# Head norms by token rows in the attention stage, and four smaller reorderings, in a two-layer encoder step

## The reference

```python
def _rms(x, g):
    y = xf * lax.rsqrt(jnp.mean(xf * xf, axis=-1, keepdims=True) + EPS)
    return (y * g).astype(x.dtype)
# in _diff_attention, eight heads, each 128 wide
p = jax.nn.softmax(jnp.where(mask, s + bias, NEG_BIG), axis=-1)
a = p[:, :, 0] - lam * p[:, :, 1]
o = jnp.einsum('bhqk,bkhe->bqhe', a, v_all)
o = _rms(o, head_g) * (1 - lam_init)
return o.reshape(B, T, D_MODEL) @ w_o
```

## Time and profile before

| what | us |
|---|---|
| median of three runs | 1470.3 (1469.63 to 1471.16) |
| the profiled execution | 1470.15 |
| its span, first to last instruction | 1468.4 |
| PE busy | 1444.8 |
| PEld busy | 1368.3 |
| DVE busy | 1048.7 |
| POOL busy | 759.3 |
| ACT busy | 427.6 |

### The profile page before, as it was taken

The page is one execution under the profiler, slowest core; times in us unless marked ns, Lnnn a source line. Parts: engine busy times, 40 slices in busy tenths (PEclk is TensorE's granted clock), DMA queues, the critical chain, the costliest instruction groups (busy, mean ns, idle before and its releaser), DMA issues.

```text
span 1468.4 us, 29233 instructions
## 1 busy us (share of the span) xinstructions
PE 1444.8 (98%) x11236; PEld 1368.3 (93%) x11236; DVE 1048.7 (71%) x1862; ACT 427.6 (29%) x906; POOL 759.3 (52%) x513
## 2 busy tenths in 40 slices
PE   6999999999999999999999999999999999999999
PEld 4987899999999999999999887778999999999998
DVE  5897665567776877776688347886966779476698
ACT  5303454211110011112232147774421133111132
POOL 2445343555555455555545444567565556555554
PEclk9999999999999999999999999999999999999999
DMA  9573222244456544444222252231222222222222
GB/s 377 177 254 133 89 87 74 87 157 151 166 200 214 194 144 162 153 169 138 83 92 72 84 190 89 89 103 38 79 85 73 86 94 79 89 84 86 86 90 104
DMA packets 57531, 183.50 MB, mean 125 GB/s; under 512 B 6440, under 2 KB 9904, under 8 KB 57440
## 3 DMA queue, kind: packets, MB, share of 16 engines
q1 hardware_dynamic: 54432, 179.25, 35.7%
q10 hardware_dynamic: 3008, 3.01, 0.6%
HBM read 171.69 MB, written 10.55 MB: 124 GB/s over the span
## 4 chain that ended last, share of the span: by engine, by line
PE 90%; DVE 5%; issue 1%; DMA 1%; ACT 1%; POOL 0%; SPq 0%; ACTq 0%; DVEq 0%; POOLq 0%
PE psum L779 62%; PE psum L845 7%; PE psum L1054 7%; PE psum L1253 3%; PE psum L1345 1%; PE psum L1188 1%; DMA ada_first<-in_ada_w 1%; PE psum L1308 1%; PE psum L1060 1%; DVE w_ring L2581 1%; DVE act_lo L2013 1%; PE psum L1295 1%; PE psum L1291 1%; PE psum L790 1%; PE psum L816 1%
## 5 line engine op out<-in xcount | busy, mean ns | idle before, releaser
L658 POOL TENSOR_SCALAR w_hi<-raw 128x1024 fp32r<-128x1024 f32 (+1 forms) x168 | 192.0, 1143 | 574.4 <-PE psum L779 478.3
L662 POOL TENSOR_TENSOR w_lo<-raw,w_hi 128x1024 fp32r<-128x1024 f32 (+2 forms) x195 | 440.5, 2264 | 14.0
L779 PE MATMUL psum<-act_hi,w_hi 128*128 128x288 f32 (+1 forms) x1952 | 424.8, 299 | 1.3 <-issue 0.6
L779 PE MATMUL psum<-act_hi,w_lo 128*128 128x288 f32 (+1 forms) x1952 | 420.9, 297 | 0.0
L779 PE MATMUL psum<-act_lo,w_hi 128*128 128x288 f32 (+1 forms) x1952 | 420.5, 297 | 0.0
L779 PEld LDWEIGHTS psum<-act_hi,w_hi 128*128 128x128 f32 x1952 | 315.5, 190 | 6.4 <-issue 4.0
L779 PEld LDWEIGHTS psum<-act_hi,w_lo 128*128 128x128 f32 x1952 | 316.0, 189 | 0.0
L779 PEld LDWEIGHTS psum<-act_lo,w_hi 128*128 128x128 f32 x1952 | 315.3, 189 | 0.0
L779 PE MATMUL psum<-hid_both,w_hi 128*128 128x288 f32 x704 | 122.9, 297 | 0.0
L1960 DVE SCALAR_TENSOR_TENSOR psum<-ada_quad,cst,psum 128x512 f32<-128x512 f32 x168 | 112.8, 748 | 0.0
L779 PEld LDWEIGHTS psum<-hid_both,w_hi 128*128 128x128 f32 x704 | 103.5, 189 | 1.2 <-issue 1.2
(11 more groups left out here) (383 smaller groups left out, 2457.2 us busy)
## 6 DMA issues: line engine op xcount, KB each, us to landing
raw<-in_w_stream SPq DMA_DIRECT2D x153, 512.0 KB, 3.5
ada_quad<-in_ada_w SPq DMA_DIRECT2D x56, 512.0 KB, 4.5
raw<-in_w_down SPq DMA_DIRECT2D x32, 704.0 KB, 4.1
ada_first<-in_ada_w SPq DMA_DIRECT2D x8, 1024.0 KB, 14.2
ada_ring<-in_ada_w SPq DMA_DIRECT2D x14, 512.0 KB, 4.4
ada_more<-in_ada_w SPq DMA_DIRECT2D x10, 512.0 KB, 5.3
line_rep<-line SPq DMA_DIRECT2D x8, 352.0 KB, 4.5
line<-line_rep SPq DMA_DIRECT2D x8, 352.0 KB, 5.2
```

The costliest lines, as they stand in the source:

```text
L658: pool.tensor_scalar(hi, src, 1.0, 0.0, ALU.mult, ALU.add).then_inc(hi_split, 1)
L662: last = pool.tensor_tensor(lo[:, c:c + w], src[:, c:c + w], hi[:, c:c + w].bitcast(F32), ALU.subtract)
L779: last = mm(psum[:, b + half, 0:n_cols], weights[wp][:, k, :], parts[ap][:, k, half * HT:half * HT + n_cols], start=(k == 0 and n == 0), s ...
```

## The change

**Attention.** `att_values` swaps its operands, so a head's output comes out with tokens on partitions: a block is 128 tokens by 128 features. The sum of squares is then ScalarE's own accumulation (`out_squares`: five Square instructions, then Identity, Ln and Exp on 128x5). VectorE makes the root (`out_root`, three instructions on 128x5), which stands in step 3 behind `att_score` and ahead of `att_weight`; ScalarE scales the four prompt blocks (`out_norm`), VectorE the sample block (`out_norm`, behind `att_weight`); TensorE turns the five tiles back (`out_turn`, step 4) and ScalarE copies them to SBUF (`out_back`). `att_sums`, `att_sums_sample` and GpSimd's nine instructions per head go. The heads alternate between PSUM banks 5 and 6. In the tail, `out_turn` of head 7 stands ahead of the last `out_part`, and the eight pieces of output unit 4 run in another order on other banks.

```diff
                     pool.memset(bias_p[(h + 1) % 2][0:64, 448:512], NEG).then_inc(mask_ready, 1)
                 if h == H - 1:
                     split_unit(U_AO + 3)
-                if h >= 1:
-                    z, y, t, o = (tmp[:, n, :] for n in (1, 2, 3, 5))
-                    pool.wait_ge(oy_ready, h)
-                    pool.wait_ge(oz_ready, 2 * h)
-                    if 2 <= h <= 3:
-                        pool.wait_ge(lo_ready[A_O], 1)
-                    elif h >= 4:
-                        pool.wait_ge(sc_mm, 5 * h + 5)
-                    if h == 1:
-                        pool.wait_ge(kv_stored, 192)
-                    def by_half(out, a, b):
-                        pool.tensor_tensor(out[:, 0:HT], a[:, 0:HT], b[:, 0:HT], ALU.mult)
-                        return pool.tensor_tensor(out[:, HT:T], a[:, HT:T], b[:, HT:T], ALU.mult)
-
-                    steps(by_half(t, y, y))
-                    steps.wait()
-                    steps(by_half(t, t, z))
-                    steps.wait()
-                    steps(pool.tensor_scalar(t, t, -0.5, 1.5, ALU.mult, ALU.add))
-                    steps.wait()
-                    steps(by_half(t, t, y))
-                    steps.wait()
-                    by_half(o_place[h - 1][:, :], t, o).then_inc(ov_ready, 1)
-                    pool.wait_ge(ov_ready, h)
             split_pairs(121, 2)
             def sum_blocks(hf, n):
...
-                if h >= 1:
-                    pe.wait_ge(o_out, h)
+                if qt == 0 and h >= 2:
+                    pe.wait_ge(ov_ready, h - 1)
+                if qt == 0 and 1 <= h < H - 1:
...
                     for kt in range(5):
                         n = P if kt < 4 else TS
                         w = vc_sb[h % 2][:, kt, :] if kt < 4 else v_sb[h // 4][0:TS, 4, h % 4 * P:(h % 4 + 1) * P]
-                        last = mm(psum[:, 4, 448:512], w, atr[0:n, g % 2, kt * DK:(kt + 1) * DK], start=(kt == 0), stop=(kt == 4))
+                        last = mm(psum[0:TS, 4, 384:512], atr[0:n, g % 2, kt * DK:(kt + 1) * DK], w, start=(kt == 0), stop=(kt == 4))
                 last.then_inc(av_done, 1)
 
-            def att_sums(h):
-
-                pe.wait_ge(osq_ready, h + 1)
-                pe.wait_ge(kz_ready, min(2 * H, H + h + 3))
-                if h >= 1:
-                    pe.wait_ge(oz_ready, 2 * h)
-                mm(psum[:, 6, :], mean_sq, tmp[:, 0, 0:TP], start=True, stop=True)
-
-            def att_sums_sample(h, late=False):
-
-                pe.wait_ge(o_out, h + 1)
-                pe.wait_ge(at_ready, min(5 * H, 5 * h + 6 + late))
-                mm(psum[:, 4, 448:512], mean_sq, tmp[:, 0, TP:T], start=True, stop=True).then_inc(oms_ready, 1)
+            def out_turn(h):
+
+                pe.wait_ge(hn_act, H + h + 1)
+                pe.wait_ge(hn_dve, H + h + 1)
+                pe.wait_ge(at_ready, min(5 * H, 5 * h + 7))
+                for j in range(4):
+                    pe.transpose(psum[:, o_bank(h), j * P:(j + 1) * P], hn[j], ident)
+                pe.transpose(psum[:, 4, 448:512], hn[4], ident[0:TS, 0:TS]).then_inc(o_turned, 1)
 
             def out_part(f):
...
+                elif s == 4 and p >= 1:
+                    out_turn(p - 1)
...
-            att_sums_sample(H - 1)
             for f in parts:
+                if f == 15:
+                    out_turn(H - 1)
                 out_part(f)
             pe.wait_ge(lo_split, U_AO + 5)
             pe.wait_ge(o_half_read, 12)
-            pe.wait_ge(o_out, H)
-            pe.wait_ge(oz_ready, 2 * H)
-            for k, j in ((0, 0), (0, 1), (1, 0), (1, 1), (2, 0), (3, 0), (2, 1), (3, 1)):
+            pe.wait_ge(ov_ready, H - 1)
+            for k, j in ((0, 0), (1, 0), (2, 0), (0, 1), (1, 1), (2, 1), (3, 0), (3, 1)):
                 if j == 0:
                     pe.wait_ge(lo_ready[A_O], 5 + k)
-                last = out_tile(4, j, k, 4 + 2 * j, k == 0, k == 3)
+                elif k == 0:
+                    pe.wait_ge(ov_ready, H)
+                last = out_tile(4, j, k, o_banks[j], k == 0, k == 3)
                 if (k, j) == (3, 0):
                     last.then_inc(o_done, 1)
...
             def out_sample(h):
                 sa.wait_ge(av_done, 5 * h + 5)
                 if h >= 1:
-                    sa.wait_ge(ov_ready, h)
-                af(tmp[:, 5, TP:T], psum[:, 4, 448:512], ACT.Copy)
-
-            def out_prompt(h):
-                af(tmp[:, 5, 0:TP], psum[:, 5, :], ACT.Copy).then_inc(o_out, 1)
+                    sa.wait_ge(hn_dve, H + h)
+                af(o_sample, psum[0:TS, 4, 384:512], ACT.Copy).then_inc(o_out, 1)
+
+            def out_squares(h):
                 sa.wait_ge(o_out, h + 1)
-                if h >= 1:
-                    sa.wait_ge(oms_ready, h)
-                af(tmp[:, 0, :], tmp[:, 5, :], ACT.Square).then_inc(osq_ready, 1)
-
-            def z_sample(h):
-                sa.wait_ge(oms_ready, h + 1)
-                if h >= 1:
-                    sa.wait_ge(ov_ready, h)
-                af(tmp[:, 1, TP:T], psum[:, 4, 448:512], ACT.Identity, bias=EPSC, scale=D / P).then_inc(oz_ready, 1)
-
-            def z_prompt(h):
-                af(tmp[:, 1, 0:TP], psum[:, 6, :], ACT.Identity, bias=EPSC, scale=D / P).then_inc(oz_ready, 1)
-
-            def head_guess(h):
-                sa.wait_ge(oz_ready, 2 * h + 2)
-                steps(af(tmp[:, 2, :], tmp[:, 1, :], ACT.Ln))
+                for j in range(TT):
+                    src = psum[:, o_bank(h), j * P:(j + 1) * P] if j < 4 else o_sample
+                    n = P if j < 4 else TS
+                    last = af(hn[j], src, ACT.Square, accum_out=ssq[0:n, j:j + 1])
+                steps(last)
                 steps.wait()
-                af(tmp[:, 2, :], tmp[:, 2, :], ACT.Exp, scale=-0.5).then_inc(oy_ready, 1)
+                steps(af(z5, ssq, ACT.Identity, bias=EPSC, scale=1.0 / P))
+                steps.wait()
+                steps(af(y5, z5, ACT.Ln))
+                steps.wait()
+                af(y5, y5, ACT.Exp, scale=-0.5).then_inc(oy_ready, 1)
+
+            def out_norm(h):
+                sa.wait_ge(of_ready, h + 1)
+                for j in range(4):
...
                     ts_(selr[:, h % 2, :], cst[:, C_SEL2:C_SEL2 + DK], r[:, 0:1], VEC, ALU.mult, ALU.mult).then_inc(weighted, 1)
 
+            def out_root(h):
+                ve.wait_ge(oy_ready, h + 1)
+                if h >= 1:
+                    ve.wait_ge(hn_act, H + h)
+                newton(y5, z5, t5, f5).then_inc(of_ready, 1)
+
+            def out_norm(h):
+                ve.wait_ge(of_ready, h + 1)
+                ts_(hn[4], o_sample, f5[0:TS, 4:5], None, ALU.mult).then_inc(hn_dve, 1)
+
             def head_lo(h):
                 ve.wait_ge(hi_ready[A_O], h + 1)
...
                     query_first(p + 2)
-                elif s == 4 and p + 3 < H:
+                elif s == 4 and 1 <= p < H - 3:
                     query_second(p + 2)
                 elif g == 5 * (H - 2):
                     query_second(H - 1)
+                if s == 3 and p >= 1:
+                    out_root(p - 1)
                 if g >= 1:
                     att_weight(g - 1)
+                if s == 3 and p >= 1:
+                    out_norm(p - 1)
                 if g == 3:
                     kq_scale(H + 1, tmp[:, 5, :])
+                    query_second(2)
                 elif s == 2 and 1 <= p < H - 1:
```

```diff
+            def split_behind(u0, but_last_used):
+
+                pool.wait_ge(raw_in[u0 % 2], 16 * (u0 // 2 + 1))
+                but_last_used()
+                for k0, k1 in ((0, KT - 1), (KT - 1, KT)):
+                    src = raw[:, u0 % 2, k0 * P:k1 * P]
+                    hi, lo = (w_parts[u0 % 2][part][:, k0:k1].rearrange("p k c -> p (k c)") for part in range(2))
+                    if k1 == KT:
+                        pool.wait_ge(unit_done, u0 - 1)
+                    last = pool.tensor_scalar(hi, src, 1.0, 0.0, ALU.mult, ALU.add)
+                    if k1 < KT:
+                        steps(last)
+                        steps.wait()
+                    else:
+                        last.then_inc(hi_split, 1)
+                        pool.wait_ge(hi_split, u0 + 1)
+                    if k1 < KT:
+                        pool.wait_ge(lo_ready[A_HN], H)
+                    last = pool.tensor_tensor(lo, src, hi.bitcast(F32), ALU.subtract)
+                last.then_inc(lo_split, 1)
+
...
-            split_pairs(3, 26)
+            split_pairs(3, (U_OUT - 1) // 2)
+            split_behind(U_OUT + 2, lambda: pool.wait_ge(turned, H))
+            split_unit(U_OUT + 3)
+            split_pairs(U_OUT + 4, 2)
+            split_unit(U_FFN0, pieces=4)
+            split_unit(U_FFN0 + 1)
```

(10 more changed lines are left out.)

102 lines of the change are left out of this document (45 added, 57 removed).

## The result

| | before | after |
|---|---|---|
| median | 1470.3 (1468.41 to 1471.16) | 1477.51 (1477.06 to 1479.72) |
| ratio | | 1.0052, 95% interval 1.0042 to 1.0063 |
| the profiled execution, its span | 1470.15, 1468.4 | 1479.72, 1477.9 |

The change makes the kernel 7.2 us slower; the forecast was 2.2 us, its range ended 0.5 us under the measured median. The profiled execution lies 2.2 us over its own median. S of a head is the start of TensorE's scores of step 2, as in the prediction.

The account below looks back on a forecast made before the run. It took TensorE, 90% of the chain, as the bound. Mixer -1.7, heads 1 to 4 +3.6, later heads and tail +0.4 gave +2.3 us on 1470.15: forecast 1472.5, its own range 1469.5 to 1475.5, overall 1466 to 1477.

Parts of the forecast that it names:

- the values keep their products: TensorE in a head: swapping the operands of the values was taken to leave their products as they were.
- the 1.4 named as a sign: Heads 1 to 4: TensorE's weight transposes of block 3 would wait about 1.4 us for VectorE, once a head.
- The even case of 4 x 0.48 us gained: Heads 1 to 4, in the faster rival: the root's wait is hidden, giving 4 x 0.48 us; 1463 in all, chance 0.13.
- the term of +0.85: Head 5: out_turn waits for ScalarE's scalings from S+8.7 to S+10.95, moving the turn of block 3 by +0.85 us.
- -0.3, since the wait of block 3 behind a long split piece shrinks: Head 7: the 1.2 us wait of block 3 behind a long split piece would shrink, for -0.3 us.
- the unit boundary: Tail: +0.45 us, as unit 4's first half ends 0.8 us instead of 1.6 before the second, its residual taking 1.1.
- The wait of 0.5 us that the tail was to lose: Tail: a TensorE wait of 0.5 us was to be gone, part of the tail's -0.5 us.
- The k-tile: Mixer, ahead of the heads: six products of 0.13 us each fill TensorE's wait, for -0.75 us.
- the state DMAs: Mixer: four DMA issues less ahead of ScalarE's squares bring them 1.8 us forward, for -0.2 us.
- The early split: Mixer's output units: the split of seven k-tiles starts some 4 us earlier, ending TensorE's idle 0.62 us, for -0.75 us.
- A wait that is removed can't cost: Mixer: the claim that its terms, together -1.7 us, could not turn into a loss; the gain ends at -1.8.
- the waits add up: Slower rival: out_turn late by 1.3 us or more delays block 3's turn, 2.5 us per 0.5 in five heads; 1477, chance 0.2.

Follow-up runs that it names:

- split_late: The changed kernel, with GpSimd's split in heads 1 to 4 waiting until VectorE has ended the weights of block 3: 1475.63 us.
- comb: The changed kernel with later head_hi, root, out_turn and splits of heads 1 to 4, head 7's split in four low pieces, GpSimd's mixer order of before: 1471.64 us.
- short_hold: The changed kernel, with the low part of the unit split in head 7 cut from one GpSimd instruction into four: 1475.81 us.
- both_late: The changed kernel, with head_hi of heads 5 to 7 behind step 3's scalings and the low part of head 7's split unit in four pieces: 1473.11 us.
- mixer_only: The kernel before, with the change's GpSimd and mixer parts and nothing of the attention: 1469.47 us.
- mixer_no_behind: The kernel before, with the change's mixer part only (k-tile ahead of the heads, earlier state DMAs), GpSimd's order as before: 1469.89 us.
- filler: The changed kernel, with eight repeated score products added to TensorE ahead of the long out_turn waits in each of heads 5 and 7: 1475.55 us.

## Why the prediction was right or wrong

**Heads 1 to 4: right, +3.6 forecast, +3.55 measured.** The two steps that carry it hold. The root waits for ScalarE for 1.23 us (1.15 forecast), and the low pieces run under the weights of block 3 and cost 0.64 us (0.66 forecast). So VectorE frees TensorE at S+14.39 (14.4 forecast). TensorE's own steps were off and it didn't show: `out_turn` waited 0.44 us, five transposes took 0.79 (0.65 taken; the earlier trace rows had said 0.78), and "the values keep their products" was wrong for the sample, whose products are now 128 wide and not 64: +0.16. Without any wait for block 3, as in split_late, TensorE turns it at S+13.75 and not at 13.03, so the wait there was 0.6 us and not the 1.4 named as a sign. The even case of 4 x 0.48 us gained was never there: with both causes and the wait of `out_turn` mended (comb) the four heads take 78.85 us, 0.12 a head under before. That the sum agrees to 0.05 us is luck: by the scatter of these heads it could as well have been +2.8 or +4.3. One reading was not borne out by its row: the scores at 904.14 in the earlier trace rows ran behind the split, which ended at 903.61 in the earlier trace rows, so they say nothing on whether scores are held beside it. Nothing in the sum used this.

**Head 5: the wait right, its price wrong.** The forecast of 2.25 us (10.95 less 8.7) was 2.19 measured. The step that failed is the term of +0.85: it priced a wait at its own length. With the clock up the same head takes 21.3 us (split_late), +1.15; in the profiled execution it took 22.7 (+2.6), and up to 24.2 in another kernel. The prediction read the granted clock of the earlier trace rows and took it as given for the stretches that it made idle; the runs show 1.4 us more behind this wait, for 3.4 us at half clock.

**Head 7: wrong.** "-0.3, since the wait of block 3 behind a long split piece shrinks" followed the long instruction only to the place where it had stood. With the norm's nine instructions gone from GpSimd and the scaling new on VectorE, it met the scaling. 1.6 us of wait (3.1 in the place of 1.5) and 1.35 of clock came of it, and short_hold and both_late give these 2.95 us back. The tail missed the same thing at a smaller price, 0.35 us, and the unit boundary cost 0.7 where 0.45 was taken. The wait of 0.5 us that the tail was to lose did not stand there: of the two waits for VectorE's x in the kernel before, 0.48 us lay in head 6 (at 988.12) and 0.33 in head 7 (1012.78), none in the tail.

**The mixer: -1.7 forecast, -0.6 measured.** The k-tile gave 0.59 (0.75), because its six products took 1.0 us there and not 0.8; the state DMAs gave 0.32 (0.2). The early split failed, -0.75 forecast and +0.4 measured (mixer_only against mixer_no_behind). The sentence "PE began a unit late since the split came late" was right, but what comes next was not asked. It was the residual on VectorE, 0.08 us behind, and the long low part itself made it later. "A wait that is removed can't cost" is thus wrong of this term: the early low part removed one wait and held VectorE ahead of the next.

**The sum.** From 2.3 to 7.9 us in the traces (behind the start, which has nothing of the change): 1.1 in the mixer, 2.75 at half clock, 1.6 of wait in head 7, 0.3 in head 5 with the clock up, 0.35 at head 7's turn in the tail, 0.25 at the unit boundary, 0.5 for the wait that wasn't in the tail, 0.15 less in heads 1 to 4 and 6, and -1.1 in head 0 and at the end, which is mostly scatter. The rival "the waits add up" named 1477, but by another way: it wanted `out_turn` late by 1.3 us in heads 1 to 4, where it is late by 0.44.

## What to carry to other kernels

Where TensorE is the bound and its clock is up, a wait that a change opens is priced too low at its own length: here one of about 2 us cost up to 2.9 us more. So split it, or give TensorE its next work ahead of it. When work leaves GpSimd, its long instructions move, so list what VectorE does beside each of them at the new place; cutting one such instruction into four costs GpSimd 0.4 us here (2.52 to 2.96) and took 1.6 us off what it held (2.36 to 0.74). And when a late input is brought forward, name the next thing that the consumer waits for before booking the gain.

## What was not expected of the hardware

- The granted clock fell to half for 3.4 us, or for twice that, behind waits of 1.9 to 4.0 us and behind one pair of 0.8 and 1.5, in some executions and not in others at the same wait. 3.4 us of it cost 1.4 us here. With more work on TensorE (filler) it stayed up.
- A VectorE operation of 128x5 or 128x12 elements took 2.24 and 1.84 us beside one GpSimd subtraction of 2.4 and 2.1 us, and 0.17 without it: what such an instruction costs VectorE doesn't depend on how small VectorE's own is.
- Where two engines go through the same pattern unit after unit, their places against each other decide whether VectorE's pair takes 1.6 or 3.25 us in all of them: it begins 1.55 us behind GpSimd's low part in the one case and 0.46 us ahead of it in the other.
